# Projections of a hybrid decoder layer: weight slots reloaded once split, high parts made three products ahead

## The chip, the cores and the metric

The kernel runs on one core of a Trainium2 chip. The metric is the device time of one execution in microseconds (us), as the median of several runs. The core has five engines that work through lists of their own and meet at semaphores: TensorE (PE, matrix products), VectorE (DVE), ScalarE (ACT), GpSimd (POOL) and SyncE (SP), which here issues all transfers between HBM and the on-chip memory SBUF. Products are summed in PSUM banks.

## The reference

One decoder layer over 2048 tokens of width 1024. The change touches only its first stage: the norm, the input projection, and the pointwise work that prepares four mixers.

```python
hn = rmsnorm(h, mix_norm[l])
a_q, a_f, a_i, a_g, b_y, b_x, c_u, d_z = jnp.split(hn @ w_in[l], IN_SPLITS, axis=-1)
y_a = hgrn2_mixer(a_q, a_f, a_i, a_g, lb_all[l], hg_norm[l])
y_b = rglru_mixer(b_y, b_x, ...)
y_c = s5_mixer(c_u, ...)
y_d = rwkv7_mixer(d_z, ...)
h = h + jnp.concatenate([y_a, y_b, y_c, y_d], axis=-1) @ w_out[l]
h = h + cross_attention(...)
h = h + conv_ffn(...)
```

w_in has 1024 x 2688 entries: 21 column tiles of 128.

## The kernel before

The first stage is project_and_prepare. The tokens go in four blocks of 512 (p = 0 to 3). In each block TensorE makes 21 products (n = 0 to 20, in the order of FEATURES: the latents, k, r, v of the RWKV part, then bx, by, f, q, g, and the four tiles a_v and c_u, which are turned to token order afterwards). Each product takes 8 contraction tiles, and each of these three matmuls: full precision is kept by splitting both operands into a high and a low part, and computing high x high, high x low, low x high (L430).

A weight tile passes three stations, each a ring of WR = 3 slots: SyncE loads it raw into w_ring (load_w, L242), ScalarE rounds it into w_high (high, L474), GpSimd subtracts and writes w_low (L349, signal w_split). The tokens of a block come twice: as they are into x_tok, from which ScalarE forms the mean squares (squares, L457), and turned into x_turned, which VectorE scales (normed) and which are split into hn_high (high_tokens, ScalarE) and hn_low (low_tokens, VectorE). x_tok and x_turned have one buffer each, so the next block's tokens are loaded and normed while the present block's products run. The scale reaches all partitions by a small product (spread_rstd), which TensorE does behind product 17.

Every engine has one list, written out by hand, and waits stand in it. On ScalarE the list of a block is run: take(n) evacuates product n from one of three PSUM banks (L495); between the takes stand the evacuations of small products (take_small, L499), the squares of the next block, and behind take 14 a long chain of sigmoid, exp, log and tanh for the decays, ending in norm_root (L478), which the next block's scale needs. Before each take of product n stands the high part of weight n + 2:

```python
def take(n, dst, func=ACT.Copy):
    if n + 2 < NF:
        high(p, n + 2)
    elif has_next:
        high(p + 1, n + 2 - NF)
```

TensorE's small products stand behind products 6 (six with the lora weights, into the two banks aux_a), 9, 10, 11, 14 and 15, and behind 16 and 17, where a v tile is turned into the bank aux_v (L402) once VectorE has emptied it (dve_bank_free). VectorE empties aux_v for the turned v tiles in v_tok (L703), in its list behind two scans (L693) and six operations (L697 to L700) that prepare the RG-LRU part.

On SyncE, load_w(n) waits for product n - 3. A block's results stay in SBUF until its end; dve_end (signalled by L726) says that all are there, and the next block's list stores them in five groups of five (store, L266), each behind one weight load. ScalarE too waits for dve_end before it starts on the next block. The last block has its own order of stores, store_last (L274, L278). load_constants also prepares ten small columns from parameters (prepare_on_act, prepare_on_dve) ahead of the first block.

## Time and profile before

| | |
|---|---|
| median of 3 runs | 3383.22 us (3381.42 to 3389.78) |
| profiled execution | 3390.33 us, span 3388.5 us |
| first stage (project_and_prepare) | 0 to about 651 us of the span |
| TensorE busy over the span | 3097.9 us (91%) |
| mean granted clock of TensorE | 0.956 |

The profile is of one execution. In its views a row gives the start, the time taken, the engine, the line, and out<-in by the names of the program; in brackets stands how long the engine had stood idle and what ended that. A busy TensorE need not run at full speed: the granted clock says which share of full speed it had.

### The profile page before, as it was taken

The page shows a single profiled execution, that of the slowest core. Times are in us where ns is not written, and L with a number is a line of the kernel's source. Part 1 is how long each engine was busy: PE and PEld are TensorE (multiplying, and loading weights), DVE is VectorE, ACT ScalarE, POOL GpSimd, SP SyncE. Part 2 cuts the span into 40 slices and gives each one's busy share as a digit, 9 for nine tenths or more (in the row PEclk, how much of TensorE's full clock was granted, in tenths as well). Part 3 has the DMA queues.
Part 4 walks back from the last instruction along what each step waited for, and adds up shares of the span by engine and source line. Part 5 has one row for each costly group of instructions (what it writes and reads, how often), then busy time and mean ns, then how long its engine had stood idle before and what let it go on. Part 6 is the DMA issues. An engine that isn't in the chain of part 4 may idle for free. (4 is left out here: it accounts for less than half of the span.)

```text
span 3388.5 us, 51366 instructions
## 1 busy us (share of the span) xinstructions
PE 3097.9 (91%) x20672; PEld 2535.5 (75%) x20672; DVE 2179.2 (64%) x3314; ACT 1332.8 (39%) x2135; POOL 500.9 (15%) x650
## 2 busy tenths in 40 slices
PE   7898979589999879998999969999899999899998
PEld 6676667488888768876888748888688887678876
DVE  5656665577764667734445467777877776577776
ACT  5646454445553131102233333333433333344443
POOL 3333333266661001100000000000000000000000
PEclk9999989789998989998999979999899999999999
DMA  5263525512210154431111132324333234667764
GB/s 182 86 205 102 179 92 158 169 63 70 78 59 18 50 190 161 152 106 38 62 68 59 48 129 106 118 106 143 106 110 114 106 116 146 214 197 222 236 204 145
DMA packets 200072, 416.20 MB, mean 123 GB/s; under 512 B 15280, under 2 KB 99504, under 8 KB 193456
## 3 DMA queue, kind: packets, MB, share of 16 engines
q1 hardware_dynamic: 199856, 413.18, 37.1%
q8 instruction: 152, 2.49, 0.3%
q14 instruction: 64, 0.52, 0.0%
HBM read 295.66 MB, written 117.46 MB: 122 GB/s over the span
## 5 line engine op out<-in xcount | busy, mean ns | idle before, releaser
L2768 PE MATMUL ffn_ps<-ffn_t_p,ffn_w_p 128*128 128x512 f32 x3696 | 848.8, 392 | 43.9 <-DVE ffn_w_p L2944 28.2
L2768 PEld LDWEIGHTS ffn_ps<-ffn_t_p,ffn_w_p 128*128 128x128 f32 x3696 | 699.6, 189 | 193.1 <-DVE ffn_w_p L2944 29.9
L2783 PE MATMUL ffn_ps<-ffn_t_p 128*128 128x512 f32 x2112 | 491.6, 395 | 24.8 <-DVE ffn_t_p L3090 18.5
L2783 PEld LDWEIGHTS ffn_ps<-ffn_t_p 128*128 128x128 f32 x2112 | 399.9, 191 | 116.5 <-DVE ffn_t_p L3090 25.0
L430 PE MATMUL proj<-hn_high,w_high 128*128 128x512 f32 x672 | 283.1, 421 | 64.8 <-ACT t_ag L495 32.0
L349 POOL TENSOR_TENSOR w_low<-w_ring,w_high 128x1024 fp32r<-128x1024 f32 x84 | 215.7, 2572 | 412.2 <-ACT w_high L474 412.2
L430 PE MATMUL proj<-hn_low,w_high 128*128 128x512 f32 x672 | 268.6, 400 | 0.0
L430 PE MATMUL proj<-hn_high,w_low 128*128 128x512 f32 x672 | 268.3, 399 | 0.0
L2794 ACT ACTIVATE ffn_w_p<-ffn_w_p_sums 128x512 fp32r<-128x512 f32 x176 | 111.1, 631 | 379.2 <-DVE ffn_w_p_sums L2965 379.1
L3090 DVE TENSOR_TENSOR ffn_t_p<-ffn_ring,ffn_t_p 128x1536 fp32r<-128x1536 f32 x88 | 154.7, 1758 | 131.9 <-ACT ffn_t_p L2864 131.5
L2864 ACT ACTIVATE ffn_t_p<-ffn_ring 128x1536 fp32r<-128x1536 f32 x88 | 131.0, 1488 | 266.8 <-DVE ffn_ring L3086 262.7
L430 PEld LDWEIGHTS proj<-hn_high,w_high 128*128 128x128 f32 x672 | 130.7, 195 | 102.0 <-ACT t_ag L495 40.1
L430 PEld LDWEIGHTS proj<-hn_low,w_high 128*128 128x128 f32 x672 | 130.9, 195 | 32.7 <-issue 6.5
L430 PEld LDWEIGHTS proj<-hn_high,w_low 128*128 128x128 f32 x672 | 130.3, 194 | 28.7
L474 ACT ACTIVATE w_high<-w_ring 128x1024 fp32r<-128x1024 f32 x84 | 88.9, 1058 | 154.1 <-DMA w_ring<-in_w_feat 134.0
L2944 DVE TENSOR_TENSOR ffn_w_p<-ffn_w_p_sums,ffn_w_p 128x512 fp32r<-128x512 f32 x176 | 120.4, 684 | 0.0
L2944 DVE TENSOR_TENSOR ffn_w_p<-ffn_ring,ffn_w_p 128x512 fp32r<-128x512 f32 x132 | 90.4, 685 | 32.3 <-ACT ffn_w_p L2794 32.3
L1981 PE MATMUL ps_w<-w_out_high,mix_high 128*128 128x512 f32 x256 | 106.2, 415 | 0.0
L2382 ACT ACTIVATE s_junk<-s_x 128x1024 f32<-128x1024 f32 x32 | 33.7, 1052 | 182.7 <-DVE s_x L2462 177.2
L2350 PE MATMUL ps_score<-key_w_high,hn_t_high 128*128 128x512 f32 x256 | 103.6, 405 | 1.1 <-DVE hn_t_low L2450 1.1
L2350 PE MATMUL ps_v<-val_w_high,prob_t_high 128*128 128x512 f32 x256 | 103.1, 403 | 0.0
L2794 ACT ACTIVATE ffn_w_p<-ffn_ring 128x512 fp32r<-128x512 f32 x132 | 82.3, 624 | 50.7 <-PE ffn_ps L2768 50.7
(477 smaller groups left out, 5858.9 us busy)
## 6 DMA issues: line engine op xcount, KB each, us to landing
ffn_ring<-in_w_up SPq DMA_DIRECT2D x44, 1024.0 KB, 5.4
ffn_ring<-in_w_down SPq DMA_DIRECT2D x88, 512.0 KB, 5.3
w_ring<-in_w_feat SPq DMA_DIRECT2D x84, 512.0 KB, 3.6
ffn_ring<-scratch_values SPq DMA_DIRECT2D x88, 257.0 KB, 4.5
scratch_gates<-ffn_gate SPq DMA_DIRECT2D x44, 512.0 KB, 2.6
ffn_ring<-scratch_gates SPq DMA_DIRECT2D x88, 256.0 KB, 3.8
feats<-scratch_scan SPq DMA_DIRECT2D x16, 896.0 KB, 4.5
scratch_values<-ffn_raw SPq DMA_DIRECT2D x22, 513.0 KB, 3.6
```

Source lines behind the costliest of these rows:

```text
L349: pool.tensor_tensor(w_low[:, n % WR], w_ring[:, n % WR], w_high[:, n % WR], ALU.subtract).then_inc(w_split.sem, 1)
L430: mm = pe.matmul(proj[:, n % 3], lhs, rhs[:, k], start=k == i == 0, stop=k == KT - 1 and i == 2)
L474: act.activation(w_high[:, n % WR], w_ring[:, n % WR], ACT.Copy).then_inc(w_high_ready.sem, 1)
L1981: mm = pe.matmul(ps_w[:, u, half], mix[u][a][:, k], w[b][:, k, half * D_HALF:(half + 1) * D_HALF], start=k == a == b == 0, stop=k == KT - ...
L2350: mm = pe.matmul(ps[:, half], lhs[a][:, k], rhs[b][:, k, half * TB:(half + 1) * TB], start=k == a == b == 0, stop=k == KT - 1 and a == 1)
L2382: act.activation(s3_junk[:], buffer(c)[:], ACT.Square, accum_out=ms[:]).then_inc(S[ss].sem, 1)
L2768: mm = pe.matmul(bank(name, s), w_part(name, a)[:, k * P:(k + 1) * P], t_part(name, b)[:, k * TB:(k + 1) * TB], start=k == a == b == 0, st ...
L2783: mm = pe.matmul(ps[:, DOWN_BANKS[2 * t + c]], down_part(n, x)[:, HID + t * TC:HID + (t + 1) * TC], down_part(n, y)[:, c * DH:(c + 1) * DH ...
L2794: act.activation(w_part(name, 0), src, ACT.Copy).then_inc(w_high[name], 1)
L2864: act.activation(down_part(n, 0), slot(("down", n))[:, 0:VAL], ACT.Copy).then_inc(down_high, 1)
L2944: dve.tensor_tensor(w_part(name, 1), src, w_part(name, 0), ALU.subtract).then_inc(w_split[name], 1)
L3090: dve.tensor_tensor(down_part(n, 1), slot(("down", n))[:, 0:VAL], down_part(n, 0), ALU.subtract)\
```

## The change

Four orders are altered; no instruction of arithmetic is added or dropped.

- SyncE: load_w(n) waits for the split of weight n - 3 (w_split), no longer for product n - 3. The load of weight 3 stands ahead of the wait for dve_end. The next block's first tokens are loaded behind the first group of stores, its other tokens at n = 7, 10, 13 (before: 12, 15, 17), and x_turned in four pairs at n = 8 to 11 (before: all eight tiles at the block's start).
- ScalarE: the high part of weight n + 3 stands behind take(n); three are made ahead of the first block. The four squares of the next block stand behind takes 2 and 5, before take 9 and before take 13 (before: before takes 9, 11 and 13, and in the chain).
- The constants are prepared within the first block.
- In the last block root_b stands before take 20.

```diff
-            def load_x_turned(p):
-                for k in range(KT):
+            def load_x_turned(p, tiles=range(KT)):
+                for k in tiles:
...
-                if has_next:
-                    sp.wait_ge(*wide_ready.at(p))
-                    load_x(p + 1, 0)
-                    sp.wait_ge(*hn_ready.at(p))
-                    load_x_turned(p + 1)
-                if has_before:
-                    sp.wait_ge(*dve_end.at(p - 1))
-                    left = list(results(p - 1))
                 for n in range(WR, NF + (WR if has_next else 0)):
 
-                    sp.wait_ge(*proj_done.at(p, n - WR))
+                    sp.wait_ge(*w_split.at(p, n - WR))
                     load_w(n % NF)
-                    if has_next and n in (12, 15, 17):
-                        j = (12, 15, 17).index(n)
+                    if has_before and n == WR:
+                        sp.wait_ge(*dve_end.at(p - 1))
+                        left = list(results(p - 1))
+                    if has_before and n < WR + 5:
+                        store(left[(n - WR) * 5:(n - WR + 1) * 5])
+                    if has_next and n == WR:
+                        sp.wait_ge(*wide_ready.at(p))
+                        load_x(p + 1, 0)
+                    if has_next and n in (7, 10, 13):
+                        j = (7, 10, 13).index(n)
                         sp.wait_ge(*sumsq.at(p + 1, j))
                         load_x(p + 1, j + 1)
-                    if has_before and n < WR + 5:
-                        store(left[(n - WR) * 5:(n - WR + 1) * 5])
+                    if has_next and 8 <= n < 12:
+                        sp.wait_ge(*hn_ready.at(p))
+                        load_x_turned(p + 1, range((n - 8) * KT // 4, (n - 7) * KT // 4))
...
                 def take(n, dst, func=ACT.Copy):
-                    if n + 2 < NF:
-                        high(p, n + 2)
-                    elif has_next:
-                        high(p + 1, n + 2 - NF)
                     if n == NF - 1 and has_next:
                         high_tokens(p + 1)
                     act.wait_ge(*proj_done.at(p, n))
                     own.done(act.activation(dst, proj[:, n % 3], func), proj_out, n)
+                    if n + WR < NF:
+                        high(p, n + WR)
+                    elif has_next:
+                        high(p + 1, n + WR - NF)
...
                     take(n, z[:, n, 1:])
+                    if has_next and n in (2, 5):
+                        squares(p + 1, (2, 5).index(n))
                     if n == 3:
...
+                        if p == 0:
+                            C["prepare_on_act"](act)
...
                 if has_next:
-                    squares(p + 1, 0)
+                    squares(p + 1, 2)
...
-                if has_next:
-                    squares(p + 1, 1)
                 for t in range(G2):
                     take(11 + t, T["f"][:, t])
                 if has_next:
-                    squares(p + 1, 2)
+                    squares(p + 1, 3)
...
+                if p == 0:
+                    act.wait_ge(C["prepared"], 1)
...
-                if has_next:
-                    squares(p + 1, 3)
...
                 for m in range(2 * G2):
+                    if m == 2 * G2 - 2 and not has_next:
+                        root_b()
...
-                    if m == 2 * G2 - 2 and not has_next:
-                        root_b()
...
-            high(0, 1)
-            C["prepare_on_act"](act)
-            act.wait_ge(C["prepared"], 1)
+            for n in range(1, WR):
+                high(0, n)
             blocks(run)
...
+                if p == 0:
+                    C["prepare_on_dve"](dve)
```

ScalarE in block 0, from the evacuation of product 14 (t_q) to that of product 15 (the first t_ag<-proj), with w_high<-w_ring for a high part and x_tok for the squares. Before:

```order
L495 ACTIVATE t_q<-proj 128x512
L543 ACT_TABLE_LOAD
L543 ACTIVATE t_k<-t_f 128x1024
...
L554 ACTIVATE t_e<-t_e 128x1024
L457 ACTIVATE x_tok,mean_sq<-x_tok 128x1024
L558 ACTIVATE t_ag<-t_ag,derived 128x512 x2
L561 ACT_TABLE_LOAD
L561 ACTIVATE t_gr<-t_gr,derived 128x512 x2
L478 ACT_TABLE_LOAD
L478 ACTIVATE rstd<-mean_sq 128x4
L474 ACTIVATE w_high<-w_ring 128x1024
L495 ACT_TABLE_LOAD
L495 ACTIVATE t_ag<-proj 128x512
```

And now:

```order
L492 ACTIVATE t_q<-proj 128x512
L475 ACTIVATE w_high<-w_ring 128x1024
L548 ACT_TABLE_LOAD
L548 ACTIVATE t_k<-t_f 128x1024
...
L559 ACTIVATE t_e<-t_e 128x1024
L561 ACTIVATE t_ag<-t_ag,derived 128x512 x2
L564 ACT_TABLE_LOAD
L564 ACTIVATE t_gr<-t_gr,derived 128x512 x2
L479 ACT_TABLE_LOAD
L479 ACTIVATE rstd<-mean_sq 128x4
L492 ACT_TABLE_LOAD
L492 ACTIVATE t_ag<-proj 128x512
```

The high part of weight 17 has moved from the chain's end to its head, and the squares have left it.

ScalarE in block 1, from the evacuation of product 4 to the small evacuations (t_decay, t_a, t_dg) of the lora products; z<-proj is an evacuation. Before:

```order
L474 ACTIVATE w_high<-w_ring 128x1024
L495 ACTIVATE z<-proj 128x512
L474 ACTIVATE w_high<-w_ring 128x1024
L495 ACTIVATE z<-proj 128x512
L474 ACTIVATE w_high<-w_ring 128x1024
L495 ACTIVATE z<-proj 128x512
L499 ACTIVATE t_decay<-aux_a,prm_sb 128x512 x2
```

And now:

```order
L492 ACTIVATE z<-proj 128x512
L475 ACTIVATE w_high<-w_ring 128x1024
L492 ACTIVATE z<-proj 128x512
L475 ACTIVATE w_high<-w_ring 128x1024
L458 ACTIVATE x_tok,mean_sq<-x_tok 128x1024
L492 ACTIVATE z<-proj 128x512
L475 ACTIVATE w_high<-w_ring 128x1024
L500 ACTIVATE t_decay<-aux_a,prm_sb 128x512 x2
```

Between the high part of weight 8 and the first small evacuation stand now the squares and the high part of weight 9 too.

SyncE at the start of block 1, from the loads of the block before to the second group of stores (t_q to t_e is the first group). Before:

```order
L235 DMA x_tok<-in_x 128x1024
L239 DMA x_turned<-in_x_t 128x512 x8
L242 DMA w_ring<-in_w_feat 128x1024
L266 DMA scratch_scan<-t_q 128x4x128 x2
L266 DMA scratch_scan<-t_k 128x4x128 x2
L266 DMA scratch_scan<-t_e 128x4x128
L242 DMA w_ring<-in_w_feat 128x1024
L266 DMA scratch_scan<-t_e 128x4x128
```

And now:

```order
L242 DMA w_ring<-in_w_feat 128x1024 x11
L266 DMA scratch_scan<-t_q 128x4x128 x2
L266 DMA scratch_scan<-t_k 128x4x128 x2
L266 DMA scratch_scan<-t_e 128x4x128
L235 DMA x_tok<-in_x 128x1024
L242 DMA w_ring<-in_w_feat 128x1024
L266 DMA scratch_scan<-t_e 128x4x128
```

The first tokens have moved behind the first stores, x_turned is gone from here, and weight 3 is the last of the eleven loads ahead of the stores.

## Rows read from the trace of the kernel before

**Rows 1.** The page, part 5, costliest groups: busy, mean, idle before.
```profile
L430 PE MATMUL proj<-hn_high,w_high 128*128 128x512 f32 x672 | 283.1, 421 | 64.8 <-ACT t_ag L495 32.0
L349 POOL TENSOR_TENSOR w_low<-w_ring,w_high 128x1024 fp32r<-128x1024 f32 x84 | 215.7, 2572 | 412.2 <-ACT w_high L474 412.2
```

**Rows 2.** Timeline, TensorE, products 17, 18, block 1's first; block 2's transposes.
```profile
140.99 0.77 PE L430 MATMUL proj<-hn_high,w_high 128*128 128x512 f32 x1 [10.66 <-ACT t_ag L495]
...
149.11 0.61 PE L402 MATMUL aux_v<-cst,z 128*128 128x128 f32 x4
...
150.37 0.48 PE L430 MATMUL proj<-hn_high,w_high 128*128 128x512 f32 x1
...
155.93 0.60 PE L417 MATMUL aux_a<-cst,t_a 128*128 128x128 f32 x4
...
169.81 0.47 PE L430 MATMUL proj<-hn_high,w_high 128*128 128x512 f32 x1 [1.49 <-DVE hn_low L629]
...
464.89 0.66 PE L402 MATMUL aux_v<-cst,z 128*128 128x128 f32 x4 [0.64 <-DVE v_tok L703]
```

**Rows 3.** Windows: PE, PEld, DVE, ACT, POOL busy, granted clock, DMA share, GB/s.
```profile
130.00:140.00 10.00, 0.33 (x3) 0.09 (x1) 6.23 (x12) 9.85 (x13) 2.53 (x1) 0.64 0.18 52
...
188.00:204.00 16.00, 16.00 (x65) 13.18 (x66) 10.51 (x15) 7.57 (x9) 7.14 (x3) 0.91 1.11 333
...
211.00:216.00 5.00, 5.00 (x24) 4.14 (x23) 3.31 (x4) 1.20 (x2) 2.40 (x1) 1.00 1.09 380
```

**Rows 4.** Timeline, TensorE, block 1: products 2 and 3, third lora product.
```profile
187.88 0.77 PE L430 MATMUL proj<-hn_high,w_high 128*128 128x512 f32 x1 [4.70 <-POOL w_low L349]
...
194.80 0.39 PE L430 MATMUL proj<-hn_high,w_high 128*128 128x512 f32 x1
...
219.83 3.95 PE L372 MATMUL aux_a<-z,lora_sb 128*128 128x512 f32 x8 [1.39 <-ACT t_decay L499]
```

**Rows 5.** Timeline, ScalarE, block 0: take 14 and the squares in the chain.
```profile
117.24 0.60 ACT L495 ACTIVATE t_q<-proj 128x512 f32<-128x512 f32 x1 [0.19 <-PE proj L430]
...
129.77 1.06 ACT L457 ACTIVATE x_tok<-x_tok 128x1024 f32<-128x1024 f32 x1
```

**Rows 6.** Timeline, VectorE and GpSimd, block 0: low parts, scans to v_tok.
```profile
137.47 6.63 POOL L349 TENSOR_TENSOR w_low<-w_ring,w_high 128x1024 fp32r<-128x1024 f32 x2 [17.96 <-ACT w_high L474]
137.49 4.45 DVE L693 TENSOR_TENSOR_SCAN t_e<-cst,t_e 128x512 f32<-128x512 f32 x2
...
138.74 3.19 DVE L693 TENSOR_TENSOR_SCAN t_e<-cst,t_e 128x512 f32<-128x512 f32 x1
141.97 2.68 DVE L697 TENSOR_TENSOR t_inv<-t_decay 128x512 f32<-128x512 f32 x1
...
148.32 0.69 DVE L703 COPY v_tok<-aux_v 128x512 f32<-128x512 f32 x1
```

**Rows 7.** Timeline, block starts: dve_end's instructions, high parts 4 and 8, loads.
```profile
182.64 1.54 DVE L726 SCALAR_TENSOR_TENSOR t_gi<-t_gi,prm_sb,t_inv 128x512 f32<-128x512 f32 x2
...
194.27 1.06 ACT L474 ACTIVATE w_high<-w_ring 128x1024 fp32r<-128x1024 f32 x1 [4.48 <-DMA w_ring<-in_w_feat]
...
211.31 5.79 SPq L242 DMA_DIRECT2D w_ring<-in_w_feat  x2
...
217.51 1.06 ACT L474 ACTIVATE w_high<-w_ring 128x1024 fp32r<-128x1024 f32 x1 [5.32 <-DMA w_ring<-in_w_feat]
...
340.03 1.54 DVE L726 SCALAR_TENSOR_TENSOR t_gi<-t_gi,prm_sb,t_inv 128x512 f32<-128x512 f32 x2
...
376.07 1.06 ACT L474 ACTIVATE w_high<-w_ring 128x1024 fp32r<-128x1024 f32 x1 [5.32 <-DMA w_ring<-in_w_feat]
```

**Rows 8.** Timeline, end of the stage: root_b, the stores of cu and yb.
```profile
640.75 0.63 ACT L503 ACTIVATE t_inv<-t_inv 128x512 f32<-128x512 f32 x1
...
642.03 0.37 SPq L278 DMA_DIRECT2D scratch_cu<-tok  x1
...
646.44 0.93 SPq L274 DMA_DIRECT2D scratch_late<-t_gi  x2
```

1 line of the change is left out of this document (removed).

## Prediction

> **Names.** The first stage runs 21 products in each of four blocks; "product 17 of block 1" is pass n = 17 of TensorE's loop with p = 1 (both count from 0). T is the end of a block's last DVE instruction (dve_end, L726), after which the next block's outputs may go out and ScalarE may begin on it. All figures are us; positions are from the span's start.
>
> **What bounds the kernel now.** I read the page's costliest groups first. The high x high matmuls of L430 take 283.1 and are the only group of their line with idle time ahead, 64.8; GpSimd waits 412.2 for ScalarE's high parts, but it is no bottleneck, so that wait costs nothing by itself [rows 1]. The change touches only this stage, so the question is where TensorE stops in it. The timeline of TensorE gives few places, and they repeat. Before product 17 it stands 10.66, and the product then takes 8.12 (140.99 to 149.11) where the next, product 18, takes 5.56 (150.37 to 155.93): 2.56 more at a low clock [rows 2]. The windows agree: the granted clock is 0.64 of full speed in 130 to 140, where TensorE is idle for all but the first third of a microsecond (so it falls to the 1.2 GHz level within that wait), and 1.00, 2.4 GHz, in the full stretch at 211 to 216 [rows 3]. Before product 0 of block 1 stand 1.48 [rows 2]; before its product 2 4.70, and that product takes 6.92 (187.88 to 194.80) where product 18 took 5.56, 1.36 more [rows 2, 4]. Before the third small product with the lora weights, 1.39 [rows 4]. Blocks 2 and 3 look like block 1.
>
> **What the change removes.** Products 2 and 17 wait for their own weights' low part, whose high part ScalarE makes late: for product 17 GpSimd gets it at 137.47 [rows 6], after the long chain of exponentials and logarithms that begins at 117.84, behind the evacuation of product 14 [rows 5]. The changed order makes it ahead of that chain; that of product 2 comes in the block before. Both waits for weights go. Read naively, that is 3 x (4.70 + 1.36) + 3 x 10.66 + the last block's like wait, some 60. I count on nearly none of it, because of what is late next.
>
> **Product 17: what is late next.** Behind product 17 in TensorE's order stand the transposes of v (L402), which write the one bank aux_v and so need the copy v_tok of the first half (L703) done. The trace shows this dependence: in block 2 the transposes waited for it after a cold product 17 [rows 2]. In block 0 that copy ends at 148.32 + 0.69 = 149.01, product 17 at about 149.1: today the product is run while VectorE works through its chain. With the change product 17 starts at 130.3, ends at 135.8, and TensorE then stands until the copy, some 14. Is the copy sooner? Its chain starts at the root (L478). On ScalarE, in front of it, the high part of weight 17 is new (1.06) and the last squares, 1.06 too [rows 5], are gone: nothing moves. From 137.49 to 148.32 VectorE runs two scans and six operations. The first scan takes 4.45 - 3.19 = 1.26, the second 3.19; the first multiply 2.68, where an operation of this size takes 0.69: 1.9 + 2.0 = 3.9 of waiting, while GpSimd makes two low parts in 6.63 [rows 6]. With the change the two low parts in that stretch are those of weights 18 and 19; the first is asked for at 139.4 (its high part is ready one 1.06 sooner than now), in the second scan, the next right behind. Two full waits of 2.35 each (a low part takes 2.57 on average, waits included [rows 1]) instead of 3.9 make the copy 0.8 later; one wait alone would make it 1.5 sooner. I take +0.8, since the rows now show two waits in a row [rows 6]. Then transposes and product 18 begin as in block 0 (1.26 apart [rows 2]), but product 18 is now the cold one: its end is at 149.01 + 0.8 + 0.1 + 1.26 + 5.56 + 2.56 = 159.3 against 155.93, **3.4 later**. Of this 1.5 comes back: the wait before product 0 of the next block is for low tokens held up behind VectorE and GpSimd, and TensorE now comes 3.4 later to them. Net **+1.9**, bounds -0.7 (one wait) to +3.4 (nothing comes back), in three blocks: **+5.7**.
>
> The Trainium skill (SBUF — State Buffer, SBUF: two separate sides) says the port pair of VectorE and GpSimd is an exclusive lock held for a whole instruction, and that a DVE operation with two SBUF inputs is subject to it. The long scan and multiply here agree (3.19 and 2.68); by that rule both low parts would cost VectorE a whole instruction each, +0.8, and what decides between one and two waits is only who comes first.
>
> **Block start: what is late next.** At T = 182.64 + 1.54 = 184.18 the 25 stores of the block before may go (22 of 0.262 MB, 3 of 0.524, 7.34 MB in all), in five groups with a weight load of 0.524 MB between. The transfers run at 333 GB/s at a share of 1.11 [rows 3]: they are the limit. Weight 8, the first behind all stores, is there at 217.51, T + 33.3, after 10.5 MB; ScalarE waited 5.32 for it [rows 7]. In the changed queue weight 3 is ahead of T (-0.524 MB), but tokens of the next block go between the store groups twice (+1.05 MB). So weight 8 comes 0.52 MB / 0.38 = 1.4 later (the rate of the stretch without short stores [rows 3]), T + 34.7. Then ScalarE must pass: high part 8 (1.06), the squares that are now here (1.06), the evacuation of product 6 (0.6), high part 9 (1.06, new ahead of the small products; its load, 1.05 MB further, lands at T + 37.4, in time), the first small evacuation (0.69). The third lora product starts at T + 34.7 + 4.5 = 39.2; now it starts at 219.83, T + 35.65 [rows 4]. That is **3.6 later**, and all that was won before it (product 3 at T + 4.6 rather than T + 10.6) is spent in waiting: product 4 for weight 4 (T + 10.1 as now, at 194.27 [rows 7]), and TensorE before the third lora product, some 5. A wait of 4.70 was followed by 1.36 lost at the low clock in block 1 [rows 4], and product 17's 10.66 by 2.56 [rows 2]; I take 2.0. Block 1: **+5.6**. In block 2 weight 8 comes at 376.07, T (340.03 + 1.54) + 34.5 today [rows 7], 1.2 later than in block 1, so the change adds 1.2 less: **+4.4**. Block 3 has no next tokens: 1.05 MB less than blocks 1 and 2 (2.8) and no squares (1.06), so its third lora product comes at T + 39.2 - 2.8 - 1.06 = 35.4, where block 2's place (T + 35.65 + 1.2) stands for today's: -1.4, with 1.9 for the clock **+0.5**. Bounds of the three: 0 and 2.6 for the clock each time, so +5 to +12.
>
> The Trainium skill (DMA: Bandwidth & Descriptors, Specifications) gives 512 B as enough for full rate; the stores have 512 B rows, and the trace disagrees: 333 GB/s with them, 380 without. At 380 throughout, weight 8 would come at about T + 31.6; this is the faster rival's page.
>
> **The rest.** In block 0 high part 9 stands ahead of the small evacuations (1.06) and the wait for the constants at the start is gone; no wait of TensorE over 0.6 is there: 0, bounds -1.1 and +1.1. The constants' work (three table loads on ScalarE, ten tiny operations on VectorE) falls between products 3 and 8, where both have room: 0. **Last block:** no squares leave the chain, so high part 17 makes it 1.06 longer; the copy is some 1.8 later, but today's product 17 ends 1.8 behind the copy, so what remains is the cold product 18, **+2.7** (0 to +4). At the stage's end the root (640.75) stood behind the evacuation of product 20; moved ahead, the last store follows that of cu (642.03 + 0.37) instead of starting at 646.44 [rows 8]: **-4.0** (-4 to -2). The stages behind are not touched.
>
> **Sum.** 0 + 5.7 + 5.6 + 4.4 + 0.5 + 2.7 - 4.0 = **+14.9**. The profiled execution took 3390.33 (span 3388.5), so 3405.2; the median of the three runs is 7.1 lower, so I forecast **3398**. Its own range takes about half of each term's way to its bounds, since they won't all fall to one side: 3385 to 3410.
>
> **Rivals.**
> - One wait instead of two for VectorE: the low part of weight 18 gets in before the first multiply, that of 19 after the copy. 4 x 2.35 less: +5.5, **3389**, no measurable change. For it: the first request comes 0.7 before the scan ends only. Against: now both hit.
> - Faster: the loads at block start had spare room. They are issued exactly at products' ends today (211.31, behind the product's end [rows 7]); once they are not paced so, the transfers may move up. If weight 8 comes before about T + 31.3, the sum is zero, 3383; with the block starts winning their 4.70 + 1.36 each (18.2) in place of +10.5, the sum is -13.8, **3369**. Against: share 1.11 already [rows 3], and it would need 11 MB in about 29, where only stretches without stores reach 380 GB/s.
> - Worse: nothing of product 0's wait comes back and product 4's stop costs a clock drop that reaches product 6: +25, **3409**.
> - That product 17's wait simply ends (-40) needs the copy v_tok off its place; the diff leaves it there, so I give it 2%.
>
> **How the numbers follow.** Forecast 56%, one wait 22%, worse 9%, faster 11%, the last 2%. 0.3% of this kernel, 10.2, is about what a measurement can tell from no change. The forecast's own range lies mostly above 3393.4 (a tenth of its chance below). So faster 0.14, same 0.24, slower 0.62. The range 3380 to 3411 leaves out the faster rivals and a tail above.
>
> **What would show it.** Right: no wait of TensorE before products 2 and 17, one of some 13 to 14 before the transposes L402 (now L403), released by v_tok; product 18 at half clock; ScalarE waiting for weight 8 until about T + 34.7 in blocks 1 and 2, and TensorE some 5 before the third lora product. Wrong: v_tok's copy before 147.5 in block 0, or weight 8 before T + 32.

## The result, and the profile after

The changed kernel took **3398.07 us** (median of 7 runs, 3389.64 to 3400.03); the kernel before, on the same chip, 3383.22 (7 runs, 3378.71 to 3389.78). The ratio is 1.0035, with a 95% interval of 1.0025 to 1.0045: slower by about a third of a percent, 14.85 us between the medians, where +14.9 was forecast.

The two profiled executions don't show this in their totals. The one of after is the fastest of its seven (3389.64, span 3387.9), that of before is slower than all seven of that kernel (3390.33, span 3388.5). The later stages, which no kernel here touches (span less the row shown next), took 2723.4 in the profile of after, 2737.5 in that of before, and between these two in all the others. So I compare the end of the stage that was changed, read in both traces where SyncE issues the first load of the next stage. In these rows SPq is SyncE's queue:

```profile
650.99 0.35 SPq L990 DMA_DIRECT2D s_raw<-in_s_raw  x1
```

```profile
664.50 0.35 SPq L994 DMA_DIRECT2D s_raw<-in_s_raw  x1
```

The first is before, the second after: **13.5 later**. I call this row's time the stage's end from here on. It is free of the scatter of the later stages, but each kernel has one trace, so its own scatter was not measured. Against the kernel before, the difference of the ends and the difference of the medians agree within 4.2 for every kernel below but one (e9: -4.7 against -12.4). A difference of a few us between two ends is therefore not clear of noise; one of 10 or more is.

The page's costliest groups of the changed kernel (part 5, as [rows 1]: busy, mean ns | idle before, releaser):

```profile
L431 PE MATMUL proj<-hn_high,w_high 128*128 128x512 f32 x672 | 281.5, 419 | 16.9 <-POOL w_low L350 10.6
L350 POOL TENSOR_TENSOR w_low<-w_ring,w_high 128x1024 fp32r<-128x1024 f32 x84 | 213.5, 2545 | 423.5 <-ACT w_high L475 423.5
```

The idle time ahead of the products fell from 64.8 to 16.9, by 48, and the stage still ends 13.5 later. The stops have moved to other instructions. TensorE's timeline at the end of block 0, as [rows 2] (start, duration, engine, line, operation, then the wait and its releaser in brackets):

```profile
131.71 0.48 PE L431 MATMUL proj<-hn_high,w_high 128*128 128x512 f32 x1
...
150.78 1.11 PE L403 MATMUL aux_v<-cst,z 128*128 128x128 f32 x4 [13.37 <-DVE v_tok L708]
...
153.26 0.77 PE L431 MATMUL proj<-hn_high,w_high 128*128 128x512 f32 x1
...
171.76 0.48 PE L431 MATMUL proj<-hn_high,w_high 128*128 128x512 f32 x1
...
634.05 1.12 PE L403 MATMUL aux_v<-cst,z 128*128 128x128 f32 x4 [9.72 <-DVE v_tok L708]
```

Product 17 starts at 131.71 with no wait. Behind it the transposes of v stand 13.37 for the copy v_tok (13.35 and 13.34 in blocks 1 and 2, 9.72 in the last). They take 1.11 instead of 0.61, and product 18's first matmul 0.77 instead of 0.48. Product 0 of block 1 (171.76) waits for nothing. The windows show the clock, with columns as in [rows 3]:

```profile
143.00:152.00 9.00, 1.22 (x6) 1.22 (x7) 7.52 (x7) 3.93 (x5) 3.75 (x3) 0.50 0.40 117
153.00:160.00 7.00, 7.00 (x32) 5.81 (x32) 6.25 (x10) 0.25 (x1) 1.15 (x1) 0.87 0.23 75
188.00:204.00 16.00, 12.10 (x45) 9.34 (x44) 7.91 (x9) 4.33 (x7) 5.98 (x3) 0.85 1.05 317
```

The granted clock is 0.50, the 1.2 GHz level, while TensorE stands, and 0.87 on average over product 18: most of that product runs at 2.4 GHz again. VectorE and GpSimd behind that stop, as [rows 6]:

```profile
139.18 2.48 DVE L698 TENSOR_TENSOR_SCAN t_e<-cst,t_e 128x512 f32<-128x512 f32 x2
141.22 5.33 POOL L350 TENSOR_TENSOR w_low<-w_ring,w_high 128x1024 fp32r<-128x1024 f32 x2 [18.17 <-ACT w_high L475]
141.69 2.66 DVE L702 TENSOR_TENSOR t_inv<-t_decay 128x512 f32<-128x512 f32 x1
144.39 2.71 DVE L703 SCALAR_TENSOR_TENSOR t_gr<-t_inv,t_gr 128x512 f32<-128x512 f32 x1
...
150.04 0.69 DVE L708 COPY v_tok<-aux_v 128x512 f32<-128x512 f32 x1
```

Both scans run free (1.24 each). The two operations behind them take 2.66 and 2.71 instead of 0.69, while GpSimd makes two low parts: two waits of 2.0. The Trainium skill (SBUF — State Buffer, SBUF: two separate sides) calls the pair's port an exclusive lock held for a whole instruction; these two rows agree.

The start of block 1, as [rows 4] and [rows 7]. T is the end of the first row's instruction, 186.11:

```profile
184.57 1.54 DVE L731 SCALAR_TENSOR_TENSOR t_gi<-t_gi,prm_sb,t_inv 128x512 f32<-128x512 f32 x2
196.48 1.06 ACT L475 ACTIVATE w_high<-w_ring 128x1024 fp32r<-128x1024 f32 x1 [8.11 <-DMA w_ring<-in_w_feat]
200.09 0.77 PE L431 MATMUL proj<-hn_high,w_high 128*128 128x512 f32 x1 [3.90 <-POOL w_low L350]
...
221.12 1.06 ACT L475 ACTIVATE w_high<-w_ring 128x1024 fp32r<-128x1024 f32 x1 [6.44 <-DMA w_ring<-in_w_feat]
224.14 1.06 ACT L475 ACTIVATE w_high<-w_ring 128x1024 fp32r<-128x1024 f32 x1 [0.44 <-DMA w_ring<-in_w_feat]
225.83 5.40 PE L373 MATMUL aux_a<-z,lora_sb 128*128 128x512 f32 x8 [4.62 <-ACT t_decay L500]
```

ScalarE waits 8.11 for weight 4 and TensorE stands 3.90 ahead of product 4 (200.09). High part 8 comes at T + 35.0, high part 9 behind it, and the third lora product at T + 39.7, after a stop of 4.62.

To see where the 13.5 lie I cut the stage at two marks that every trace has: the end of product 16, and the start of product 1 of the next block. A *tail* runs from the first mark to the second, a *block* from the second to the next product 16's end. All values are differences of rows of TensorE's timeline in the one trace of each kernel (start and duration of a product's first and last matmul), and the last column is the stage's end. "Start" runs from product 0 of block 0, at 19.8 to 20.6, to its product 16's end. Row e4 is left out, since its added matmuls overran.

| kernel | start | tails 0, 1, 2 | blocks 1, 2, 3 | last tail | stage's end |
|---|---|---|---|---|---|
| before | 110.0 | 47.2, 47.4, 47.4 | 110.0, 111.2, 110.6 | 47.3 | 651.0 |
| after | 111.6 | 47.5, 48.5, 48.0 | 115.2, 115.4, 112.2 | 46.1 | 664.5 |
| e1_vtok_early | 111.5 | 47.9, 47.8, 46.4 | 116.0, 115.8, 113.5 | 45.0 | 664.5 |
| e2_vtok_early_before | 109.9 | 46.5, 46.3, 46.1 | 111.3, 110.8, 111.0 | 47.8 | 649.6 |
| e3_small_first | 110.2 | 47.6, 48.7, 47.5 | 111.4, 113.2, 109.3 | 45.6 | 653.3 |
| e5_warm_half | 112.1 | 47.1, 47.1, 45.7 | 116.6, 116.6, 112.1 | 43.9 | 661.0 |
| e6_small_and_tokens_late | 110.9 | 48.4, 48.0, 48.4 | 108.8, 109.0, 112.0 | 46.0 | 651.7 |
| e7_loads_alone | 110.3 | 45.6, 45.5, 45.5 | 112.3, 110.1, 109.1 | 46.2 | 645.1 |
| e8_low_tokens_early | 110.5 | 44.8, 44.9, 45.2 | 114.9, 112.0, 109.3 | 43.3 | 644.9 |
| e9_three_moves | 110.5 | 44.8, 45.0, 44.9 | 111.8, 111.9, 112.6 | 45.0 | 646.3 |
| e10_loads_and_high_order | 110.4 | 49.4, 48.3, 49.7 | 112.2, 112.5, 112.7 | 49.6 | 664.9 |
| e11_weights_before_stores | 110.8 | 44.8, 45.6, 44.8 | 103.5, 103.0, 103.6 | 43.2 | 619.0 |
| e12_only_weights_first | 111.4 | 47.4, 47.5, 47.6 | 112.8, 112.6, 109.5 | 45.6 | 654.6 |

### The profile page after: what moved, and what is told of

Read it like the earlier page. It is cut to its first block and busy times, and to the rows that moved or that the text cites. A ratio compares the mean times of both kernels' runs of the same rounds, so it can differ in the third digit from the quotient of the medians.

```text
span 3387.9 us, 51366 instructions
## 1 busy us (share of the span) xinstructions
PE 3085.7 (91%) x20672; PEld 2526.0 (75%) x20672; DVE 2181.6 (64%) x3314; ACT 1334.9 (39%) x2136; POOL 498.9 (15%) x650
## 5 line engine op out<-in xcount | busy, mean ns | idle before, releaser
L2787 PE MATMUL ffn_ps<-ffn_t_p 128*128 128x512 f32 x2112 | 489.7, 394 | 26.3 <-DVE ffn_t_p L3094 19.8
L431 PE MATMUL proj<-hn_high,w_high 128*128 128x512 f32 x672 | 281.5, 419 | 16.9 <-POOL w_low L350 10.6
L2798 ACT ACTIVATE ffn_w_p<-ffn_w_p_sums 128x512 fp32r<-128x512 f32 x176 | 111.2, 632 | 378.4 <-DVE ffn_w_p_sums L2969 378.2
L2948 DVE TENSOR_TENSOR ffn_w_p<-ffn_ring,ffn_w_p 128x512 fp32r<-128x512 f32 x132 | 90.4, 685 | 32.4 <-ACT ffn_w_p L2798 32.4
```

Of the source, the lines that this page charges most:

```text
L431: mm = pe.matmul(proj[:, n % 3], lhs, rhs[:, k], start=k == i == 0, stop=k == KT - 1 and i == 2)
L2787: mm = pe.matmul(ps[:, DOWN_BANKS[2 * t + c]], down_part(n, x)[:, HID + t * TC:HID + (t + 1) * TC], down_part(n, y)[:, c * DH:(c + 1) * DH ...
L2798: act.activation(w_part(name, 0), src, ACT.Copy).then_inc(w_high[name], 1)
L2948: dve.tensor_tensor(w_part(name, 1), src, w_part(name, 0), ALU.subtract).then_inc(w_split[name], 1)
```

## The experiments

The changed kernel's parts are taken one by one first (e7, e10), then the two places that the prediction named (e1 to e6), then versions that put the findings together (e8, e9, e11, e12). The labels keep the order in which they ran.

### The parts of the change

**e7_loads_alone** is the kernel before with the raw weight's reload alone:

```diff
-                if has_before:
-                    sp.wait_ge(*dve_end.at(p - 1))
-                    left = list(results(p - 1))
                 for n in range(WR, NF + (WR if has_next else 0)):
-                    sp.wait_ge(*proj_done.at(p, n - WR))
+                    sp.wait_ge(*w_split.at(p, n - WR))
                     load_w(n % NF)
+                    if has_before and n == WR:
+                        sp.wait_ge(*dve_end.at(p - 1))
+                        left = list(results(p - 1))
```

> The kernel before with one part of the change alone: SyncE reloads a raw weight slot once it is split, instead of once its product is done. Theory: weight loads were never what TensorE waited for except behind the stores of the block before, so by itself this changes the stage's end by less than 2 either way (649 to 653) and the time is the same within 0.15%. Rival 1 (the raw loads were late in blocks 1 to 3): the stage ends 3 to 8 sooner, 3374 to 3380. Rival 2 (raw loads now get ahead of the stores' partner loads and crowd the stores): 3 to 6 later.

Measured: 3374.52 (6 runs) against 3383.64, ratio 0.9970 (0.9956 to 0.9983), stage's end 645.1, that is 5.9 **sooner**. My theory of no effect fell. The number is that of the first rival (raw loads late in blocks 1 to 3), though the place is another: of the 5.9, 5.4 lie in the three tails, at the ends of blocks 0 to 2. ScalarE's list shows why. The first row is high part 20 before, in block 0, the second is the same one in e7:

```profile
153.00 1.06 ACT L474 ACTIVATE w_high<-w_ring 128x1024 fp32r<-128x1024 f32 x1 [3.09 <-DMA w_ring<-in_w_feat]
```

```profile
150.83 1.06 ACT L474 ACTIVATE w_high<-w_ring 128x1024 fp32r<-128x1024 f32 x1
```

Before, each of the last three high parts made in a block (of weight 20 and of the next block's 0 and 1) waits 2.3 to 3.1 for its raw weight. Those waits stand in ScalarE's list ahead of the next block's high tokens, and product 0 waits for what follows from them, the 1.49 of [rows 2]. With early loads both go, and each tail is 1.7 to 1.9 shorter.

**e10_loads_and_high_order** adds one more part to e7: high part n + 3 right behind evacuation n, in place of high part n + 2 ahead of it (and so three of them ahead of the first block).

```diff
-                    if n + 2 < NF:
-                        high(p, n + 2)
-                    elif has_next:
-                        high(p + 1, n + 2 - NF)
...
                     own.done(act.activation(dst, proj[:, n % 3], func), proj_out, n)
+                    if n + WR < NF:
+                        high(p, n + WR)
+                    elif has_next:
+                        high(p + 1, n + WR - NF)
```

> e7_loads_alone plus one more part of the change: each high part is made right behind the evacuation that frees its slot (three products ahead), instead of right ahead of the next evacuation; squares, token loads and constants stay as before. Theory (the high part that now stands ahead of interleaved work delays that work: high part 9 ahead of the six small evacuations costs most, since it waits for weight 9 and the third lora product behind it): the stage ends 6 to 10 later than in e7, at 651 to 655, and what is left up to the changed kernel's 664.5 belongs to the squares and the token loads. Rival 1 (the early squares and token loads are the cost): the stage ends at 644 to 647, as e7. Rival 2 (the high parts' order is all of it): 661 to 666.

Measured: 3392.04 (10 runs) against 3381.58, ratio 1.0031 (1.0019 to 1.0042), stage's end 664.9. The second rival holds: the order of the high parts costs 19.8 against e7, and squares, tokens, constants and the moved root together change the end by 0.4 only, since they shorten the tails (49.4, 49.7 and 49.6 become 47.5, 48.0 and 46.1), and lengthen the start by 1.1 and blocks 1 and 2 by 3 each. So the change is **-5.9 for the loads, +19.8 for the order of the high parts, -0.4 for the rest**: the sum is the 13.5. By the differences of the medians the same three are -9.1, +19.6 and +4.4. The first two are clear of noise in sign and, for the order, in size; what the rest is worth can't be told from nothing.

The order is worth so much because the high parts move only past interleaved work: when evacuation n - 1 is followed directly by evacuation n, both orders are the same list. Where something stands between (the long chain between 14 and 15, the six small evacuations between 6 and 7), the high part now stands ahead of it. There product 17 runs early, and what stood behind it stops instead (the window of this view ends within the lora products, so the last row counts seven of eight):

```profile
150.63 1.11 PE L402 MATMUL aux_v<-cst,z 128*128 128x128 f32 x4 [14.35 <-DVE v_tok L704]
...
223.43 5.08 PE L372 MATMUL aux_a<-z,lora_sb 128*128 128x512 f32 x7 [3.99 <-ACT t_decay L499]
```

### The tail: the copy, the clock, VectorE's list

**e1_vtok_early** is the changed kernel with both copies of v ahead of the scans on VectorE, **e2_vtok_early_before** the kernel before with the first copy there.

```diff
+                v_to_tokens(0)
                 if has_next:
                     mean_square(p + 1)
                     diagonals(p + 1)
+                v_to_tokens(1)
...
-                for t in range(G2):
-                    dve.wait_ge(*vaux_done.at(p, 4 + t))
-                    own.done(dve.tensor_copy(v_tok[:, :, t * P:(t + 1) * P], ...), vaux_out, 4 + t)
```

> The changed kernel with one thing moved: VectorE copies v_tok, first half, before the next block's mean squares, and second half right behind the diagonals, both ahead of the scans. Theory A (TensorE stands before the transposes because of this copy alone): the stop of 13.36 in block 0 goes; transposes run right behind product 17 (about 136 to 138), product 18 starts when weight 18's low part is ready, at about 142 to 144 instead of 153.3, perhaps still cold; 8 to 9 us less in each of four blocks, of which VectorE, whose chain and low tokens are then last before product 0, gives back 1 to 3. Stage end (first load of the next stage, 664.5 with the change, 651.0 before) at 634 to 644, time 3365 to 3378, ratio to the kernel before 0.995 to 0.999. Rival B (the low parts of 18 and 19, or the chain of the decays, would hold TensorE just as long): product 18 starts at 150 or later, stage end within 3 of 664.5, ratio 1.003.

> The kernel before with the first half's v_tok copy made ahead of the next block's mean squares (the second half's at its old place). Theory A: there product 17 itself waits for its low part and ends at 149.1, no earlier than the copy did, so the copy is not on the path: stage end 651 within 2, ratio 1.000 within 0.001. Rival B2 (the copy's place costs the kernel before as much): stage end 3 or more earlier.

Measured: e1 3393.07 (5 runs) against 3381.64, ratio 1.0035 (1.0021 to 1.0049), stage's end 664.5; e2 3384.42 (10 runs), ratio 1.0010 (1.0000 to 1.0019), stage's end 649.6. In e2 the copy is not on the path, as expected. In e1 the stop goes, and nothing is won. The end is the one that rival B gave, but not by its mechanism, since product 18 does start early:

```profile
145.31 0.77 PE L431 MATMUL proj<-hn_high,w_high 128*128 128x512 f32 x1 [4.71 <-POOL w_low L350]
...
169.82 0.77 PE L431 MATMUL proj<-hn_high,w_high 128*128 128x512 f32 x1 [4.98 <-DVE hn_low L631]
```

```profile
166.90 7.00 DVE L631 TENSOR_TENSOR hn_low<-x_turned,hn_high 128x512 fp32r<-128x512 f32 x8
```

Product 18 starts 8 sooner than in after (145.31 against 153.26), and product 0 then waits 4.98 for the low tokens, which stand at the end of VectorE's list. So the copy is what TensorE waits for, but not what bounds the tail. My step "the copy sets product 18, and product 18 sets the rest" is half of it: VectorE's list up to the low tokens was only just covered.

**e4_warm** and **e5_warm_half** fill TensorE's stop with 24 and 12 matmuls that nothing reads:

```diff
+                    if n == 17:
+                        pe.wait_ge(*x_normed.at(p))
+                        for i in range(12):
+                            pe.matmul(rstd_wide[:], ones, chunk_start, start=True, stop=True)
                     small_products(n)
```

> The changed kernel with 24 added matmuls (ones by the reset row, float32, into the bank rstd_wide, whose content is overwritten right after) between product 17 and the transposes of v, in every block; their result is used by nobody. At 0.47 each they take 11.3 of the 13.4 in which TensorE stands. Theory A (product 18 is slow because TensorE stood): product 18 and the products around it take 5.6 instead of 6.45 to 7.94, transposes and scale products 0.6 and 1.06 instead of 1.11 and 1.92; 2 to 3 earlier per block, stage end 8 to 11 earlier than 664.5. If the clock is not set by the stop: no change, or later by what the added matmuls overrun.

> The changed kernel with 12 more matmuls of float32 (128x512, into a row that nothing reads) between product 17 and the transposes of v; their result is used by nothing. In the run with 24 of them they took 20.6 us, so 12 should take about 10.3 and end inside TensorE's stop of 13.4. Theory (the low clock of product 18 costs time on the path): the clock stays full, product 18 takes 5.7 instead of 6.5 to 7.0 and the stretch from the transposes to its end 6.8 instead of 8.8 and more, so product 0 and what follows come 2.0 to 2.5 sooner in each of the three blocks with a successor, the stage ends at 656 to 659 instead of 664.5 and the time is 3390 to 3395. Rival (the tail is bound by VectorE's list up to the low tokens of the next block, and product 18's low clock lies beside it): product 0 starts where it did, within 1, and the stage ends at 662 to 666.

Measured: e4 3425.93 (4 runs), ratio 1.0130 (1.0113 to 1.0147), stage's end 692.5. One such float32 matmul takes 0.86, not the 0.47 that I had assumed, so the 24 took 20.6 and overran the stop by 7 in blocks 0 to 2 and by some 11 in the last: a failed experiment for the time. It does show the clock's price: with the clock held, the stretch from the transposes to product 18's end took 6.98 in block 0 (granted clock 1.00), against 8.9 to 9.5 in after. e5 is the mended one: 3393.70 (one run, no interval), stage's end 661.0, 3.5 sooner than after.

```profile
138.00:150.00 12.00, 10.22 (x24) 4.18 (x22) 11.08 (x13) 7.14 (x10) 5.35 (x2) 1.00 0.27 86
151.00:158.00 7.00, 6.72 (x36) 5.82 (x37) 5.98 (x10) 1.18 (x2) 2.40 (x1) 1.00 0.26 75
```

These windows of e5 show a granted clock of 1.00 in the filled stop and over product 18, where after has 0.50 and 0.87. The 3.5 lie between theory (5.5 to 8.5) and rival (up to 2.5), and the table shows why: the four tails are 0.4, 1.4, 2.3 and 2.2 shorter, 6.4 together, but the start and blocks 1 and 2 are 0.5, 1.3 and 1.2 longer. In block 0 product 0 starts 1.5 sooner (170.30 against 171.76) and ends at the same time (177.51 against 177.47), because its low tokens come at 169.32 + 7.10. The clock's price is real and in part covered by VectorE. In blocks 1 and 2 TensorE, no longer held in the tail, stands longer before the third lora product (6.44 and 6.41, where after has 4.62 and 4.71), and the small products then take 6.05 and 6.17 instead of 5.40. One trace without an interval can't say more.

### The block's start

**e3_small_first** is the changed kernel with high part 9, and the second squares, behind the six small evacuations:

```diff
                     own.done(act.activation(dst, proj[:, n % 3], func), proj_out, n)
+                    if n == 6:
+                        return
                     if n + WR < NF:
...
                 for t in range(G2):
                     take_small(4 + t, T["dg"][:, t], ACT.Copy)
+                high(p, 6 + WR)
+                if has_next:
+                    squares(p + 1, 1)
```

> The changed kernel with the high part of weight 9 behind the six small evacuations (t_decay, t_a, t_dg) instead of ahead of them, and the second squares (before: behind take 5) behind it too. Theory A (at block start ScalarE's list between weight 8 and the first small evacuation is the end of the path): the third lora product starts 2.1 earlier in blocks 1 and 2, 1.06 earlier in blocks 0 and 3; stage end 5 to 8 earlier than 664.5, time 3390 to 3394. Rival C (the transfer of weight 9 or TensorE's clock sets it): under 2 in all.

Measured: 3388.16 (8 runs) against 3381.64, ratio 1.0021 (1.0010 to 1.0032), stage's end 653.3: 11.2 sooner than after, more than expected. The third lora product of block 1 comes at T + 37.4 with a stop of 2.23 instead of 4.62, and what follows is not at the low clock:

```profile
221.95 3.95 PE L373 MATMUL aux_a<-z,lora_sb 128*128 128x512 f32 x8 [2.23 <-ACT t_decay L502]
```

The eight small products take 3.95 here and 5.40 in after. (In block 2 the stop is 4.04, and they take 5.44 here too.) This one order is worth 1.4 in the start and 2.2 to 3.8 in each block.

**e6_small_and_tokens_late** puts the next block's token loads behind the stores as well, and the squares to match:

```diff
-                    if has_next and n == WR:
+                    if has_next and n == 8:
                         sp.wait_ge(*wide_ready.at(p))
                         load_x(p + 1, 0)
-                    if has_next and n in (7, 10, 13):
-                        j = (7, 10, 13).index(n)
+                    if has_next and n in (12, 14, 15):
+                        j = (12, 14, 15).index(n)
```

> The changed kernel with the order of e3_small_first on ScalarE (high part 9 behind the six small evacuations), and the next block's four token loads behind the stores (at products 8, 12, 14, 15 of SyncE's loop instead of 6, 7, 10, 13), with their squares later to match. Theory (the raw weight 8 lands late in blocks 1 to 3 because stores and tokens are ahead of it on the DMA engines): with 1.05 MB of tokens out of its way it lands 2 to 3 us sooner, its high part and the third lora product's start follow by 1 to 2.5, and the stage ends at 648 to 651, against 653.3 of e3_small_first; time 3381 to 3386. Rival (product 3 to 8 are held by ScalarE's list and by VectorE's convolution alone): high part 8 comes sooner but the third lora product does not, the stage ends at 652 to 655, the same time as e3_small_first. Other side: the squares now stand ahead of v's evacuations, and the stage ends later than 655.

Measured: 3381.02 (10 runs) against 3383.64, ratio 0.9992 (0.9981 to 1.0002), stage's end 651.7. Blocks 1 and 2 are 2.6 and 4.3 shorter than in e3, and high part 8 starts at T + 32.4 (218.96, T = 186.53) instead of T + 35.0: the theory's step holds. The end is 0.7 above the theory's range (648 to 651), since block 3, which has no tokens to load, was 2.7 longer than in e3. The third lora product's row shows where, first e3, then e6:

```profile
540.75 3.95 PE L373 MATMUL aux_a<-z,lora_sb 128*128 128x512 f32 x8 [3.28 <-ACT t_decay L502]
```

```profile
537.24 5.40 PE L373 MATMUL aux_a<-z,lora_sb 128*128 128x512 f32 x8 [4.62 <-ACT t_decay L502]
```

It starts at T + 36.6 in e6 and at T + 35.3 in e3 (T is 500.69 and 505.48), since high part 8 began 1.3 later behind T, and the small products took 1.4 longer behind the longer stop. Why weight 8 came 1.3 later, with the same order of loads and stores in that block, is not shown.

### Putting them together

**e8_low_tokens_early**: e1's copies, e3's order, and the low tokens between the two halves of the h chain, since e1 had shown VectorE's list to be next.

```diff
                     own.done(dve.tensor_tensor(T["h"][:, t], T["h"][:, t], T["by"][:, t], ALU.mult), ...)
+                    if t == 0 and has_next:
+                        low_tokens(p + 1)
...
-                if has_next:
-                    low_tokens(p + 1)
```

> The changed kernel with three moves: v's two evacuations ahead of the scans (as e1_vtok_early), high part 9 and the second squares behind the six small evacuations (as e3_small_first), and VectorE's low tokens of the next block between the two halves of the h chain instead of behind them. Theory (after e1 the tail is bound by VectorE's list up to the low tokens): product 0 of the next block starts at 165 to 167 instead of 169.8, the sum of squares behind it and T follow, at 182 to 184 instead of 186 to 187, and since the next block's start hangs on T, the stage ends at 640 to 648 and the time is 3370 to 3380, faster than both kernels. Rival (product 0 is held by GpSimd's low part and ScalarE's high tokens as well, which come at about the same time): product 0 starts at 168 to 169, T stays within 1 of 186, and the stage ends at 650 to 654, as e3_small_first alone.

Measured: 3376.49 (12 runs), ratio 0.9977 (0.9967 to 0.9987), stage's end 644.9. As the theory had it: product 0 starts at 163.09, T is 182.79, the tails fall from 47.5 to 48.5 to about 45. So VectorE's list did bind the tail. Product 0 comes even sooner than the 165 to 167 that was expected, but most of that is lost again ahead of product 1:

```profile
172.45 3.78 PE L410 MATMUL aux_v<-t_sq,cst 128*128 128x512 f32 x4 [2.76 <-ACT t_sq L588]
```

This sum of squares needs the second half of the h chain, which now stands behind the low tokens on VectorE. TensorE waits 2.76 for it and then takes 3.78 over it, where before it took 1.88. Product 1 starts 6.0 behind product 0's end (175.24 and 169.25), where that was 1.6 before. e9 and e11 have the same row, with stops of 2.76 and 3.03.

**e9_three_moves** adds e6's late tokens to e8.

> The changed kernel with the three moves of e8_low_tokens_early and the token loads behind the stores of e6_small_and_tokens_late. In the traces so far a stretch from product 16's end to product 1 of the next block took 47.2 before, 47.5 to 48.5 with the change and 44.8 to 45.2 in e8; from product 1's start to product 16's end 110 to 111 before, 115 with the change, 109 in e6 (112 in its last block) and 112 to 115 in e8. Theory (the two gains lie on different stretches and add): 20 + 110 + 3 x 45 + 2 x 109 + 112 + 43 gives a stage end at 636 to 641, and 3362 to 3372. Rival (the DMA engines hold the block's start: with T sooner the stores begin sooner, but weight 8 lands when it did): high part 8 comes 35 to 36 behind T instead of 32.4, the stage ends at 643 to 648, and the time is that of e8, 3373 to 3379.

Measured: 3369.18 (11 runs) against 3381.58, ratio 0.9962 (0.9951 to 0.9973), stage's end 646.3. The time is in the theory's range, the stage's end in the rival's: the gains on the tails and on the blocks did not add. The two measures disagree most here: the medians say 12.4 sooner than before, the one trace 4.7. The rival's mechanism isn't there either: high part 8 starts at T + 32.8, not 35 to 36. TensorE, now further ahead, stops 4.34 before the third lora product instead of 2.40 in e6, and from there to product 7 it takes 5.4 instead of 3.4.

**e11_weights_before_stores** moves SyncE's wait for T, and the stores, behind the loads of weights 4 and 5:

```diff
-                    if has_before and n == WR:
+                    if has_before and n == WR + 2:
                         sp.wait_ge(*dve_end.at(p - 1))
                         left = list(results(p - 1))
-                    if has_before and n < WR + 5:
-                        store(left[(n - WR) * 5:(n - WR + 1) * 5])
+                    if has_before and WR + 2 <= n < WR + 6:
+                        store(left[(0, 10, 15, 20)[n - WR - 2]:(10, 15, 20, 25)[n - WR - 2]])
```

> e9_three_moves with SyncE's first stores of the block before moved behind the loads of weights 4 and 5 (the stores then go out as 10, 5, 5, 5 instead of five times 5). In e6 and e8 high part 4 waited 6.5 and 8.1 for its DMA, and TensorE stood 2.0 to 3.9 before product 4. Theory: that wait goes, product 4 follows product 3 without a stop in blocks 1 to 3, which is 2 to 3 per block; weight 8 still has all stores ahead of it and comes no sooner, so part is given back there: the stage ends 2 to 7 sooner than e9. Rival 1 (weight 8 decides the whole block start): no change against e9, within 1.5. Rival 2 (the stores end later than ScalarE's wait for them ahead of the third lora evacuations): that wait appears, and the stage ends 3 or more later than e9.

Measured: **3350.74** (5 runs, 3344.85 to 3352.39) against 3381.58, ratio **0.9906** (0.9893 to 0.9918), stage's end 619.0, which is 27 sooner than e9 and 32 sooner than before. The mechanism was expected, its size was not. The first fence is block 1 in e9, ScalarE's high parts 4 and 8 and SyncE's load of weight 8 between them; the second is e11, the same three and the lora products:

```profile
191.34 1.06 ACT L475 ACTIVATE w_high<-w_ring 128x1024 fp32r<-128x1024 f32 x1 [6.41 <-DMA w_ring<-in_w_feat]
...
208.06 1.30 SPq L242 DMA_DIRECT2D w_ring<-in_w_feat  x1
...
215.51 1.06 ACT L475 ACTIVATE w_high<-w_ring 128x1024 fp32r<-128x1024 f32 x1 [5.96 <-DMA w_ring<-in_w_feat]
```

```profile
185.17 1.06 ACT L475 ACTIVATE w_high<-w_ring 128x1024 fp32r<-128x1024 f32 x1
...
203.32 0.60 SPq L242 DMA_DIRECT2D w_ring<-in_w_feat  x1
...
208.32 1.06 ACT L475 ACTIVATE w_high<-w_ring 128x1024 fp32r<-128x1024 f32 x1 [3.03 <-DMA w_ring<-in_w_feat]
209.93 5.81 PE L373 MATMUL aux_a<-z,lora_sb 128*128 128x512 f32 x12
```

Weight 4 is there before T, and its high part no longer waits. My expectation was wrong on weight 8: with stores in groups of 10, 5, 5 and 5, its load stands ahead of the last group (five stores, 2.1 MB), not behind all. It is asked for 4.7 sooner and its high part starts 7.2 sooner, T + 25.4 for T + 32.8. The lora products then run in one piece without a stop, and a block takes 103.4. The size fits the bytes: behind T and up to weight 8's own load, e9 has 25 stores and five weight loads, 10.0 MB, and e11 20 stores and three, 6.8 MB. That is 3.15 MB fewer, of which the last five stores are 2.1 and weights 4 and 5, now ahead of T, 1.05. From T to high part 8 the windows show 322 GB/s in e9 (182.7 to 215.5) and 285 in e11 (182.9 to 208.3). The Trainium skill (DMA: Bandwidth & Descriptors, Queues, rings and completion order) says that descriptors on a DMA engine are consumed in ring order. The two traces are in line with that, since with 3.15 MB fewer ahead high part 8 begins 7.4 sooner behind T; but the load was also asked for 4.7 sooner, so they don't show it by themselves.

**e12_only_weights_first**: the changed kernel with e11's edit alone.

> The changed kernel with SyncE's edit of e11_weights_before_stores alone: the wait for T and the stores of the block before stand behind the loads of weights 4 and 5, nothing else is moved. In e11 that edit took blocks 1 to 3 (product 1's start to product 16's end) from 112 to 103.3 each. Theory (two causes in a row hold the block's start: weights 4 and 5 behind T and the stores, and behind them high part 9, which stands ahead of the six small evacuations and waits for weight 9's DMA): without the first the second still holds the third lora product at about T+35, so a block takes 107 to 111 instead of 115.3 in blocks 1 and 2, and the stage ends at 646 to 655; time 3380 to 3390. Rival 1 (the late weights were all of it): blocks at 103 to 105, stage end 630 to 637, time below 3372. Rival 2 (high part 9 was all of it, and weights 4 and 5 matter only once it is gone): blocks at 113 to 116, stage end 660 to 666.

Measured: 3389.28 (10 runs) against 3384.17, ratio 1.0017 (1.0007 to 1.0026), stage's end 654.6, in the theory's range, though blocks 1 and 2 are 112.8 and 112.6 where 107 to 111 was expected. The rows show the two causes in a row (here too the view's window ends within the lora products):

```profile
212.13 1.06 ACT L475 ACTIVATE w_high<-w_ring 128x1024 fp32r<-128x1024 f32 x1 [4.58 <-DMA w_ring<-in_w_feat]
...
221.35 1.06 ACT L475 ACTIVATE w_high<-w_ring 128x1024 fp32r<-128x1024 f32 x1 [6.64 <-DMA w_ring<-in_w_feat]
...
223.03 5.14 PE L373 MATMUL aux_a<-z,lora_sb 128*128 128x512 f32 x7 [8.96 <-ACT t_decay L500]
```

Products 4 to 6 no longer stop, and high part 8 is early here too (T + 26.2). But high part 9 stands ahead of the small evacuations and waits 6.64 for its weight, until T + 35.4. TensorE stands 8.96 there, and the third lora product starts at T + 37.1, where the theory had some T + 35. The edit of SyncE's queue is worth 2.4 to 2.8 a block with that order, and 8.3 to 9.1 in e11 against e9. Those two also have the moves of e1, e6 and e8, so that the place of high part 9 makes the difference is read from these rows and not shown by a run of its own.

## Why the prediction was right, point by point

**The forecast's frame held.** It said that of some 60 us of waits nearly nothing would be won, since other work was late next, and that the sum would be positive. The idle time ahead of the products fell by 48 and the stage ended 13.5 later, against +14.9; the medians differ by 14.85. That these last two agree to a tenth is luck: the terms below miss by up to 1.6 each.

**Product 17.** No wait before it, 13.4 before the transposes, released by v_tok: as written. Two waits of VectorE for GpSimd, as today, and not the one of the rival: as written, but each cost 2.0 where I had put 2.35. The first low part was also asked for later than forecast (141.22, not 139.4), so both scans ran free and both waits fell on the operations behind them. So the copy came 0.1 later against product 16 (1.72 in absolute time, of which 1.62 is the shift from block 0), not 0.8. The low clock cost 1.95 from the transposes to product 18's end in block 0, where I had taken 2.56 from a product that started after a stop. The sign "product 18 at half clock" came true for its first matmuls alone: it took 6.45 against 5.72, at a granted clock of 0.87. Together product 18 ended 2.0 later against product 16, not 3.4. Of that 1.7 came back before product 0, whose wait of 1.49 went; 1.5 was forecast. The term that was mis-sized is the tail: **+1.9 each forecast, +0.3, +1.1 and +0.7 measured** by the table (tail 1 has 48.5 for 47.4).

**Block starts.** High part 8 at T + 35.0 (forecast T + 34.7), the third lora product at T + 39.7 (T + 39.2), the stop before it 4.62 (some 5), product 4 held by weight 4: the best step of the prediction. By the table blocks 1, 2, 3 are **+5.2, +4.2 and +1.6, for +5.6, +4.4 and +0.5**. e3 shows the mechanism by taking it away, and e12 shows its second half, high part 9.

**Block 0** was the step that failed: 0 with bounds of 1.1, and it was **+1.6**. ScalarE and TensorE there:

```profile
61.39 1.06 ACT L475 ACTIVATE w_high<-w_ring 128x1024 fp32r<-128x1024 f32 x1
62.47 1.28 ACT L500 ACT_TABLE_LOAD   x1
63.76 1.41 ACT L500 ACTIVATE t_decay<-aux_a,prm_sb 128x512 f32<-128x512 f32 x2
64.50 3.95 PE L373 MATMUL aux_a<-z,lora_sb 128*128 128x512 f32 x8 [2.06 <-ACT t_decay L500]
```

High part 9 (1.06) stands ahead of the small evacuation, as I had said. But the constants' work, moved behind evacuation 3, leaves another table on ScalarE, and the load of 1.28 lies bare between high part 9 and the sigmoid. I had put the constants at 0 because both engines have room between products 3 and 8; I had counted their instructions and not the state they leave. In e10, which has the order but not the constants, the same stop is 0.64 instead of 2.06; in e3, which has the constants but not high part 9 there, it is 1.26. Both together made it long enough to show.

**Last block and the stage's end.** Forecast +2.7 - 4.0 = -1.3, measured -1.2: +2.2 up to product 18's end, and -3.4 behind it. The last stores follow each other as written (cu 658.41, yb 658.83).

**What I did not see.** I gave the loads at a block's start 11% as a gain, by rate: share 1.11, so no room. The rate had no room, but the order did. Reloading once split was worth 5.9 by itself (e7), most of it at the blocks' ends, where I had not looked, and it was already in the change, hidden by the 19.8 of the high parts' order. Two more loads ahead of the stores, with the loss-making order undone, give e11. The prediction weighed each part against what it would meet and never asked which part carried a gain. No rival holds "two parts of opposite sign".

**Still open.** Why weight 8 came later in e6's block 3 than in e3's, and why e9's trace shows so much less than its median, were not traced to a cause. e11 was not split further, so how its gain divides between weights 4 and 5 and the later place of the last store group is argued from rows, not shown by a run.

## What to carry to other kernels

When an instruction is made earlier in an engine's list, ask what it now stands ahead of, and for what it may wait there: a high part that waits 6 us for a DMA holds the six evacuations behind it, however free the engine is. On a saturated DMA path the order of the queue is the resource: put the loads that something waits for ahead of stores that nobody waits for, and ahead of the wait that releases the stores. And price a bundle of edits one by one: here a gain of some 6 to 9 and a loss of some 20 came in one diff.

## What was not expected of the hardware

- A float32 matmul of 128x512 takes 0.86 (24 in 20.6, e4), where one of the fp32r products that make up a projection advances by 0.23 at the same clock (products of 24 in 5.6).
- After a stop of 13.4 the first stretch (four transposes, the scale products, product 18) costs 1.95 to 2.5 more than at the full clock; after a stop of 2.23 the small products took 3.95 as they do at the full clock (e3), and after 4.62 they took 5.40. The length of the stop alone does not decide: behind a stop of 2.06 before the same products in block 0 they took 3.95 in after (granted clock 1.00 over 62 to 69) and 5.40 in e5 (0.79 over 60 to 68), and after 3.49 they took 3.95 (e8, block 3).
- A stretch that is freed of a stop can end at the same time, stop or no stop: product 0 in e5 (177.51) and in after (177.47), with the low tokens as its pace.
